# Gate and up of the feed-forwards: the high weight times both activation parts in one 512-column product, the halves added by VectorE

## The chip, the cores and the metric

The kernel runs on one core of a Trainium2 chip. The metric is device time in microseconds of that core, from one launch; the median of three runs is given. A profile is one execution recorded by the hardware profiler.

## The reference, cut to what matters

The reference is a chain of two small networks on 256 tokens of width 1024. The first is two layers of attention and Fourier mixing with modulated norms, for 256 latent and (in layer 0) 256 context tokens; the second is two layers of a recurrent mixer between two feed-forwards. What the change touches is the feed-forward, which all of them share:

```python
FFN_HIDDEN = 2816
def swiglu(h, w_gate, w_up, w_down):
    return (jax.nn.silu(h @ w_gate) * (h @ w_up)) @ w_down
```

It is computed seven times with 256 tokens each: layer 0 of the first network for the latent tokens (call 0) and the context tokens (call 1), layer 1 (call 2), and two in each layer of the second network (calls 3 to 6).

## The kernel before, in words

Activations lie with the feature on the partition: `x`, `h_hi` and so on are 128 partitions x 8 blocks (`KD`, index k) x 256 tokens (`T`). A feed-forward call runs over 22 tiles f (`FT`) of 128 hidden features. For each tile, `gate_up(f)` (L2019) makes two products of 128 hidden features by 256 tokens, gate (part 0) and up (part 1), each summed over the 8 blocks k; `down(f)` (L2035) multiplies the tile's result by 128 rows of the down weight and adds to all 8 output blocks, which stay in PSUM banks 0 to 3 for the whole call.

**Two parts for precision.** TensorE multiplies in the reduced type fp32r. To keep precision, every weight and every activation is split into a high part (rounded to fp32r) and a low part (the rest, in fp32r too), and a product is three: high by high, high weight by low activation, low weight by high activation. That is `split_product` (L2002), with one 256-column product in each of its lines L2005, L2006 and L2007:

```python
nc.tensor.matmul(out, hi, to_hi, start=start, stop=False, skip_group_check=True)
nc.tensor.matmul(out, hi, to_lo, start=False, stop=False, skip_group_check=True)
return nc.tensor.matmul(out, lo, to_hi, start=False, stop=stop, skip_group_check=True)
```

So `gate_up` is 8 x 2 x 3 = 48 products of 256 columns and `down` 8 x 3 = 24. Each comes with a load of its own weight block of 128 x 128 (PEld in the profile). Gate and up of a tile lie in the two halves of one PSUM bank, 4 + f % 2.

**The engines.** SyncE loads the weights in the order of use: `ring_a` holds two chunks of 1 MB (gate and up of one tile), `ring_d` two of 0.5 MB (`load_a` and `load_d`, L493 and L498); a slot is loaded again when `a_used` or `d_used` says that the chunk before last has been split. ScalarE rounds the high parts: `round_a` (L661, `w_hi`, two casts at L668) and `round_d` (L670, `d_hi`, L676). VectorE subtracts for the low parts: `rest_a` (L1307, `w_lo`, L1315) and `rest_d` (L1319, `d_lo`, L1322). GpSimd makes the low part of the activations, `rest_h` (L547, `h_lo`, L552), block by block ahead of a call; in `split_here` (L2009) the first tile of a call waits for each block.

**One tile.** When `gate_up(f)` is done (`gu_done`), ScalarE's `tile(f)` (L696) applies Silu to the gate half, from PSUM into `sg` (L700), and then makes the high parts of tile f+2 and of the down weight f+1. VectorE's `tile(f)` (L1346) multiplies `sg` by the up half from PSUM into `hid` (L1349, `hid_mul`), rounds it (L1353), subtracts (L1355, `hid_ready`), and then makes the low parts of the same weights. All engines work in the order of their own programs; semaphores tie them.

**TensorE's order** in a call (L2056 to L2070) is gate_up(0), gate_up(1), down(0), then gate_up(f), down(f-1) for f = 2 to 21, and down(21) last. So between the end of `gate_up(f)` and `down(f)` lie `down(f-1)` and `gate_up(f+1)`, except for the last tile, where only `down(20)` lies between. `gate_up(f)` waits for `a_used` (its weights are split) and for `hid_mul` of tile f-2 (its bank is read).

**Beside.** In calls 0 and 1, the norms of the other token set are done step by step between the first 12 tiles (`BESIDE`, L72), by `beside(f)` on all three engines; they use PSUM banks 6 and 7, as all norms do (`norm_bank`). These tiles are written out; the others are in a loop of two tiles.

Of the kernel before, what the change touches and what calls it, by code (L numbers as in the profile page):

```python
# [22 lines left out]
F32R = mybir.dt.float32r  # L23
ALU = mybir.AluOpType
# [5 lines left out]
T = 256  # L30
KD = D // P
# [142 lines left out]
def program(nc, wa, wd, c1_in, c2_in, vec_in, small_in, four_in, x_in, ctx_in, out):  # L174
    with ExitStack() as ctx:
        def sb(name, *shape, dtype=F32):
            return ctx.enter_context(nc.sbuf_tensor(name, [P, *shape], dtype))
# [25 lines left out]
        h_hi, h_lo = (sb(n, KD, T, dtype=F32R) for n in ("h_hi", "h_lo"))  # L203
# [63 lines left out]
        def const1(name):  # L267
# [58 lines left out]
            sem(n) for n in ("gu_done", "dn_done", "sg_ready", "hid_mul", "hid_rounded", "hid_ready", "ffn_out"))  # L326
        resid = sem("resid")
# [125 lines left out]
        def wait(eng, semaphore, value, i=None, step=2):  # L453

            if i is not None:
                eng.wait_ge(semaphore, i * step + value)
            elif value > 0:
                eng.wait_ge(semaphore, value)

# [138 lines left out]
        def _(act):  # L598
# [91 lines left out]
            def ffn(call, beside=None):  # L690
# [5 lines left out]
                def tile(f, i=None):  # L696
                    t = call * FT + f
                    wait(act, gu_done, t + 1, i)
                    wait(act, hid_mul, t - 1, i)
                    nc.scalar.activation(sg[:, f % 2, :], ps[:, 4 + f % 2, 0:T], ACT.Silu).then_inc(sg_ready, 1)  # L700
                    if f + 2 < FT:
                        round_a(call, f + 2, i)
                    elif call == 0:
                        round_a(1, f + 2 - FT)
                    if f + 1 < FT:
                        round_d(call, f + 1, i)
                    elif call == 0:
                        round_d(1, 0)

                alone = 2 if beside is None else BESIDE  # L710
# [515 lines left out]
        def _(dve):  # L1226
# [113 lines left out]
            def ffn(call, beside=None):  # L1340
# [5 lines left out]
                def tile(f, i=None):  # L1346
                    t = call * FT + f
                    wait(dve, sg_ready, t + 1, i)
                    nc.vector.tensor_tensor(hid[:, f % 2, :], sg[:, f % 2, :], ps[:, 4 + f % 2, T:2 * T], ALU.mult)\  # L1349
                        .then_inc(hid_mul, 1)  # L1350
# [15 lines left out]
                alone = 2 if beside is None else BESIDE  # L1366
# [560 lines left out]
        def _(pe):  # L1927
# [87 lines left out]

            def ffn(call, key, beside=None):
                c0, d0 = chunk0[f"ffn{call}"], call * FT

                def gate_up(f, i=None):  # L2019
                    c, t = c0 + f, d0 + f  # L2020
                    wait(pe, a_used, c + 1, i)
                    if f >= 2 or call:
                        wait(pe, hid_mul, t - 1, i)
# [37 lines left out]
                alone = 2 if beside is None else BESIDE  # L2061
# [666 lines left out]
```

## Time and profile before

| | |
|---|---|
| median of the three runs | 2498.73 us |
| the three runs | 2503.24, 2498.30, 2498.73 us |
| span of the profiled execution | 2501.0 us |
| time of that execution outside the span | not given separately |
| TensorE busy, mean granted clock | 2388.0 us (95%), 0.979 |
| weight loads busy | 2209.4 us (88%) |
| VectorE, ScalarE, GpSimd busy | 1287.4, 1053.8, 318.5 us |
| read from HBM | 389.46 MB |

How to read it: the span goes from the first to the last instruction. PE is TensorE's matmuls, PEld its weight loads, which run beside them; DVE is VectorE, ACT ScalarE, POOL GpSimd. A matmul's recorded duration is from its start until its last result is out, and matmuls are pipelined: the next starts while results of the one before still come. What one costs in a row is the distance between starts. `128*128 128x256` is a weight block of 128 rows by 128 columns and 256 moving columns. The clock is the share of full speed (2.4 GHz) that was granted to TensorE; it has two levels, 1.0 and 0.5. `A <-B 3.9` is idle time before A that B ended.

### The profile page before, as it was taken

The numbers are of one execution on the slowest core, as the hardware profiler recorded it, in microseconds if no ns is written. First come the engines' busy times: TensorE is split into PE (matmuls) and PEld (weight loads), VectorE is DVE, ScalarE is ACT, GpSimd is POOL, SyncE is SP. The second block draws the span as 40 slices with busy tenths as digits, with TensorE's granted clock in tenths as the row PEclk, the third lists the DMA queues.
The fourth block names the chain that finished last, engine by engine and source line by source line (L and its number), as shares of the span: only waits on it lengthen the run. The fifth ranks groups of instructions, "written<-read, shape, count | busy, mean of one in ns | idle before, by whom it ended". The sixth has DMA issues, their size and how long they took to land.

```text
span 2501.0 us, 51373 instructions
## 1 busy us (share of the span) xinstructions
PE 2388.0 (95%) x21244; PEld 2209.4 (88%) x21244; DVE 1287.4 (51%) x2054; ACT 1053.8 (42%) x1666; POOL 318.5 (13%) x263
## 2 busy tenths in 40 slices
PE   7989999999998799999999999999999999999998
PEld 3756899999975699989998889999999988989998
DVE  1053365565425255465557755555555558555554
ACT  3154444444335343343346434433433355435333
POOL 0000000000000000010014426200100125336000
PEclk9999999999999899999999999999999999999999
DMA  6255454445426355355433213645444232125542
GB/s 264 72 203 219 180 195 177 182 171 177 149 85 236 135 203 186 140 181 185 175 109 125 89 70 119 223 177 179 170 180 176 104 133 101 69 86 182 197 176 101
DMA packets 65512, 392.51 MB, mean 157 GB/s; under 512 B 7264, under 2 KB 7392, under 8 KB 28000
## 3 DMA queue, kind: packets, MB, share of 16 engines
q1 hardware_dynamic: 64224, 383.81, 42.1%
q10 hardware_dynamic: 864, 5.16, 0.5%
q8 instruction: 105, 1.72, 0.3%
q0 software_dynamic: 288, 1.57, 0.2%
q14 instruction: 31, 0.25, 0.0%
HBM read 389.46 MB, written 1.05 MB: 156 GB/s over the span
## 4 chain that ended last, share of the span: by engine, by line
PE 83%; DVE 4%; POOL 4%; issue 4%; ACT 3%; DMA 2%; POOLq 0%; SPq 0%; DVEq 0%; ACTq 0%
PE ps L2005 21%; PE ps L2006 21%; PE ps L2007 21%; PE ps L2091 5%; POOL t_lo L574 3%; PE ps L2106 2%; PE ps L2405 2%; PE ps L2546 1%; POOL h_lo L552 1%; PE ps L1975 1%; DMA ring_a<-in_wa 1%; PE ps L1952 1%; PE ps L2121 1%; DVE work L1395 1%; DMA work<-in_wa 1%
## 5 line engine op out<-in xcount | busy, mean ns | idle before, releaser
L2005 PE MATMUL ps<-h_hi,w_hi 128*128 128x256 f32 x2464 | 701.9, 285 | 7.1 <-DVE mod L1243 2.9
L2006 PE MATMUL ps<-h_lo,w_hi 128*128 128x256 f32 x2464 | 698.7, 284 | 0.0
L2007 PE MATMUL ps<-h_hi,w_lo 128*128 128x256 f32 x2464 | 698.6, 284 | 0.0
L2005 PEld LDWEIGHTS ps<-h_hi,w_hi 128*128 128x128 f32 x2464 | 474.3, 193 | 11.6 <-issue 4.6
L2006 PEld LDWEIGHTS ps<-h_lo,w_hi 128*128 128x128 f32 x2464 | 474.4, 193 | 0.1
L2007 PEld LDWEIGHTS ps<-h_hi,w_lo 128*128 128x128 f32 x2464 | 474.4, 193 | 0.0
L1315 DVE TENSOR_TENSOR w_lo<-ring_a,w_hi 128x1024 fp32r<-128x1024 f32 x308 | 366.4, 1231 | 25.3 <-ACT w_hi L668 25.2
L2005 PE MATMUL ps<-hid_hi,d_hi 128*128 128x256 f32 x1232 | 348.7, 283 | 0.0
L2006 PE MATMUL ps<-hid_lo,d_hi 128*128 128x256 f32 x1232 | 348.7, 283 | 0.0
L2007 PE MATMUL ps<-hid_hi,d_lo 128*128 128x256 f32 x1232 | 348.6, 283 | 0.0
L1349 DVE TENSOR_TENSOR hid<-sg,ps 128x256 f32<-128x256 f32 x154 | 64.9, 421 | 546.9 <-ACT sg L700 546.9
L700 ACT ACTIVATE sg<-ps 128x256 f32<-128x256 f32 x154 | 59.1, 384 | 674.4 <-PE ps L2007 674.4
L668 ACT CAST w_hi<-ring_a 128x1024 fp32r<-128x1024 f32 x308 | 306.0, 1044 | 11.8 <-DMA ring_a<-in_wa 11.8
L2005 PE MATMUL ps<-h_hi,t_hi 128*128 128x256 f32 x880 | 261.3, 297 | 17.9 <-POOL t_lo L574 10.7
L2006 PE MATMUL ps<-h_lo,t_hi 128*128 128x256 f32 x880 | 253.5, 288 | 0.0
L2007 PE MATMUL ps<-h_hi,t_lo 128*128 128x256 f32 x880 | 253.1, 288 | 0.0
L552 POOL TENSOR_TENSOR h_lo<-nsq,h_hi 128x256 fp32r<-128x256 f32 x72 | 60.7, 865 | 1446.8 <-ACT h_hi L687 853.8
L2005 PEld LDWEIGHTS ps<-hid_hi,d_hi 128*128 128x128 f32 x1232 | 236.5, 192 | 0.0
L2006 PEld LDWEIGHTS ps<-hid_lo,d_hi 128*128 128x128 f32 x1232 | 236.5, 192 | 0.0
L2007 PEld LDWEIGHTS ps<-hid_hi,d_lo 128*128 128x128 f32 x1232 | 236.5, 192 | 0.0
L574 POOL TENSOR_TENSOR t_lo<-ring_a,t_hi 128x512 fp32r<-128x512 f32 x120 | 172.6, 1462 | 314.7 <-ACT t_hi L997 314.7
L676 ACT CAST d_hi<-ring_d 128x1024 fp32r<-128x1024 f32 x154 | 161.6, 1050 | 98.4 <-PE ps L2007 98.4
(308 smaller groups left out, 3477.6 us busy)
## 6 DMA issues: line engine op xcount, KB each, us to landing
ring_a<-in_wa SPq DMA_DIRECT2D x282, 1024.0 KB, 4.8
ring_d<-in_wd SPq DMA_DIRECT2D x154, 512.0 KB, 5.3
work<-in_wa SPq DMA_DIRECT2D x6, 1024.0 KB, 22.1
work<-in_small POOLq DMA_DIRECT2D x2, 768.0 KB, 5.5
c<-in_c ACTq DMA_DIRECT2D x1, 1175.0 KB, 10.7
work<-in_c ACTq DMA_DIRECT2D x1, 1088.0 KB, 4.9
x<-in_x ACTq DMA_DIRECT2D x1, 1024.0 KB, 15.1
work<-in_ctx ACTq DMA_DIRECT2D x1, 1024.0 KB, 19.6
```

Of the source, the lines that this page charges most:

```text
L552: nc.gpsimd.tensor_tensor(h_lo[:, k, :], nsq[:, k, :], h_hi[:, k, :].bitcast(F32), ALU.subtract)\
L574: nc.gpsimd.tensor_tensor(t_lo[:, t % 2, k], ring_a[:, c % 2, t % 2, k], t_hi[:, t % 2, k].bitcast(F32), ALU.subtract).then_inc(done, 1)
L668: nc.scalar.copy(w_hi[:, f % 2, part], ring_a[:, c % 2, part]).then_inc(hi_a, 1)
L676: nc.scalar.copy(d_hi[:, f % 2], ring_d[:, d % 2]).then_inc(hi_d, 1)
L700: nc.scalar.activation(sg[:, f % 2, :], ps[:, 4 + f % 2, 0:T], ACT.Silu).then_inc(sg_ready, 1)
L1315: ins = nc.vector.tensor_tensor(w_lo[:, f % 2, part], ring_a[:, c % 2, part], w_hi[:, f % 2, part].bitcast(F32), ALU.subtract)
L1349: nc.vector.tensor_tensor(hid[:, f % 2, :], sg[:, f % 2, :], ps[:, 4 + f % 2, T:2 * T], ALU.mult)\
L2005: nc.tensor.matmul(out, hi, to_hi, start=start, stop=False, skip_group_check=True)
L2006: nc.tensor.matmul(out, hi, to_lo, start=False, stop=False, skip_group_check=True)
L2007: return nc.tensor.matmul(out, lo, to_hi, start=False, stop=stop, skip_group_check=True)
L2091: mm = nc.tensor.matmul(ps[:, 4 + p % 2, 0:cols.stop - cols.start], ring_a[:, slot, i % 2, k, :], h[:, k, cols], start=(k == 0), stop=(k = ...
L2106: mm = nc.tensor.matmul(ps[:, 4 + p % 2, b * P:(b + 1) * P], h[:, k, b * P:(b + 1) * P], ring_a[:, slot, i % 2, k, :], start=(k == 0), sto ...
```

## The change

High and low part of the activations come to lie side by side for each k (`h_parts`, 8 x 2 x 256), so that one product of the high weight with both is 512 columns wide and fills a whole PSUM bank: the first half holds high by high, the second half high weight by low activation. The product of the low weight by the high activation (256 columns) is added onto the second half. Gate and up of a tile now need a bank each: banks 4 and 5 for even tiles, 6 and 7 for odd ones. VectorE adds the two halves, with one `reduce_sum` over pairs that lie 256 elements apart for gate (into `sg`) and one for up (into `hid`); ScalarE applies Silu to `sg` in place, and VectorE multiplies in SBUF. `down` is not changed. Since banks 6 and 7 serve the norms beside calls 0 and 1, the first 12 tiles of these two calls keep the form of before; two more of their tiles are written out ahead of the loop. `wide_from[call]` is the first wide tile, 12 for calls 0 and 1 and 0 for the others.

```diff
--- before.py
+++ after.py
@@ -200,7 +200,8 @@
         vfirst = sb("vfirst", QT, T)
 
 
-        h_hi, h_lo = (sb(n, KD, T, dtype=F32R) for n in ("h_hi", "h_lo"))
+        h_parts = sb("h_parts", KD, 2, T, dtype=F32R)
+        h_hi, h_lo = h_parts[:, :, 0, :], h_parts[:, :, 1, :]
         t_hi, t_lo = (sb(n, 2, KD, P, dtype=F32R) for n in ("t_hi", "t_lo"))
         with nc.sbuf_tensor("work", [P, WORK], F32) as work:
             pass
@@ -324,6 +325,7 @@
         dn_bank, h2_lat = sem("dn_bank"), sem("h2_lat")
         gu_done, dn_done, sg_ready, hid_mul, hid_rounded, hid_ready, ffn_out = (
             sem(n) for n in ("gu_done", "dn_done", "sg_ready", "hid_mul", "hid_rounded", "hid_ready", "ffn_out"))
+        gate_summed, up_summed = sem("gate_summed"), sem("up_summed")
         resid = sem("resid")
         rope_rot, rope_sin, rope_cos, rope_out = (sem(n) for n in ("rope_rot", "rope_sin", "rope_cos", "rope_out"))
         fo_dft, fo_fu, fo_ch, fo_fm, fo_w, fo_out = (
@@ -456,6 +458,15 @@
                 eng.wait_ge(semaphore, i * step + value)
             elif value > 0:
                 eng.wait_ge(semaphore, value)
+
+        def both_parts(bank):
+            return ps[:, bank, :].rearrange("p (a t) -> p t a", t=T)
+
+        wide_from = [BESIDE if call < 2 else 0 for call in range(len(ffns))]
+        wide0 = [sum(FT - w for w in wide_from[:call]) for call in range(len(ffns))]
+
+        def gate_up_bank(f):
+            return 4 + 2 * (f % 2)
 
         def norm_bank(key):
             return 6 + n_id[key] % 2
@@ -695,9 +706,13 @@
 
                 def tile(f, i=None):
                     t = call * FT + f
-                    wait(act, gu_done, t + 1, i)
-                    wait(act, hid_mul, t - 1, i)
-                    nc.scalar.activation(sg[:, f % 2, :], ps[:, 4 + f % 2, 0:T], ACT.Silu).then_inc(sg_ready, 1)
+                    if f >= wide_from[call]:
+                        wait(act, gate_summed, wide0[call] + f - wide_from[call] + 1, i)
+                        nc.scalar.activation(sg[:, f % 2, :], sg[:, f % 2, :], ACT.Silu).then_inc(sg_ready, 1)
+                    else:
+                        wait(act, gu_done, t + 1, i)
+                        wait(act, hid_mul, t - 1, i)
+                        nc.scalar.activation(sg[:, f % 2, :], ps[:, 4 + f % 2, 0:T], ACT.Silu).then_inc(sg_ready, 1)
                     if f + 2 < FT:
                         round_a(call, f + 2, i)
                     elif call == 0:
@@ -707,7 +722,7 @@
                     elif call == 0:
                         round_d(1, 0)
 
-                alone = 2 if beside is None else BESIDE
+                alone = 2 if beside is None else BESIDE + 2
                 for f in range(alone):
                     tile(f)
                     if beside is not None:
@@ -1345,9 +1360,19 @@
 
                 def tile(f, i=None):
                     t = call * FT + f
-                    wait(dve, sg_ready, t + 1, i)
-                    nc.vector.tensor_tensor(hid[:, f % 2, :], sg[:, f % 2, :], ps[:, 4 + f % 2, T:2 * T], ALU.mult)\
-                        .then_inc(hid_mul, 1)
+                    if f >= wide_from[call]:
+                        s, bank = wide0[call] + f - wide_from[call], gate_up_bank(f)
+                        wait(dve, gu_done, t + 1, i)
+                        nc.vector.reduce_sum(sg[:, f % 2, :], both_parts(bank), AX_X).then_inc(gate_summed, 1)
+                        nc.vector.reduce_sum(hid[:, f % 2, :], both_parts(bank + 1), AX_X).then_inc(up_summed, 1)
+                        wait(dve, up_summed, s + 1, i)
+                        wait(dve, sg_ready, t + 1, i)
+                        nc.vector.tensor_tensor(hid[:, f % 2, :], sg[:, f % 2, :], hid[:, f % 2, :], ALU.mult)\
+                            .then_inc(hid_mul, 1)
+                    else:
+                        wait(dve, sg_ready, t + 1, i)
+                        nc.vector.tensor_tensor(hid[:, f % 2, :], sg[:, f % 2, :], ps[:, 4 + f % 2, T:2 * T], ALU.mult)\
+                            .then_inc(hid_mul, 1)
                     wait(dve, hid_mul, t + 1, i)
                     wait(dve, dn_done, t - 1, i)
                     nc.vector.tensor_copy(hid_hi[:, f % 2, :], hid[:, f % 2, :]).then_inc(hid_rounded, 1)
@@ -1363,7 +1388,7 @@
                     elif call == 0:
                         rest_d(1, 0)
 
-                alone = 2 if beside is None else BESIDE
+                alone = 2 if beside is None else BESIDE + 2
                 for f in range(alone):
                     tile(f)
                     if beside is not None:
@@ -2013,12 +2038,35 @@
                 else:
                     pe.wait_ge(norm_out, n_id[key] + 1)
 
+            def wide_gate_up(key, f):
+
+                for k in range(KD):
+                    if f == 0:
+                        split_here(key, k)
+                    for part in range(2):
+                        out = ps[:, gate_up_bank(f) + part, :].rearrange("p (a t) -> p a t", t=T)
+                        nc.tensor.matmul(out, w_hi[:, f % 2, part, k, :], h_parts[:, k], start=(k == 0), stop=False,
+                                         skip_group_check=True)
+                        mm = nc.tensor.matmul(out[:, 1, :], w_lo[:, f % 2, part, k, :], h_hi[:, k, :], start=False,
+                                              stop=(k == KD - 1), skip_group_check=True)
+                return mm
+
             def ffn(call, key, beside=None):
                 c0, d0 = chunk0[f"ffn{call}"], call * FT
 
                 def gate_up(f, i=None):
                     c, t = c0 + f, d0 + f
                     wait(pe, a_used, c + 1, i)
+                    if f >= wide_from[call]:
+                        s = wide0[call] + f - wide_from[call]
+                        if f < 2:
+                            wait(pe, hid_mul, t - 1)
+                        elif f == wide_from[call]:
+                            wait(pe, hid_mul, t)
+                        else:
+                            wait(pe, up_summed, s if f == wide_from[call] + 1 else s - 1, i)
+                        wide_gate_up(key, f).then_inc(gu_done, 1)
+                        return
                     if f >= 2 or call:
                         wait(pe, hid_mul, t - 1, i)
                     for k in range(KD):
@@ -2058,7 +2106,7 @@
                 if call == 1:
                     pe.wait_ge(ffn_out, 1)
                 down(0)
-                alone = 2 if beside is None else BESIDE
+                alone = 2 if beside is None else BESIDE + 2
                 for f in range(2, alone):
                     gate_up(f)
                     down(f - 1)
```

## Rows read from the trace of the kernel before

**Rows 1.** The page: busy time, and the chain that ended last, by line.
```profile
PE 2388.0 (95%) x21244; PEld 2209.4 (88%) x21244; DVE 1287.4 (51%) x2054; ACT 1053.8 (42%) x1666; POOL 318.5 (13%) x263
...
PE 83%; DVE 4%; POOL 4%; issue 4%; ACT 3%; DMA 2%; POOLq 0%; SPq 0%; DVEq 0%; ACTq 0%
PE ps L2005 21%; PE ps L2006 21%; PE ps L2007 21%; PE ps L2091 5%; POOL t_lo L574 3%; PE ps L2106 2%; PE ps L2405 2%; PE ps L2546 1%; POOL h_lo L552 1%; PE ps L1975 1%; DMA ring_a<-in_wa 1%; PE ps L1952 1%; PE ps L2121 1%; DVE work L1395 1%; DMA work<-in_wa 1%
```

**Rows 2.** Windows: stretch, its length, busy us (instructions) by engine, clock, DMA share, GB/s.
```profile
900.00:1000.00 100.00, 100.00 (x836) 100.00 (x835) 53.56 (x69) 37.68 (x46) 0.00 (x0) 1.00 0.49 178
```

**Rows 3.** Timeline of TensorE: start us, duration us, engine, line, operation.
```profile
1203.21 0.28 PE L2006 MATMUL ps<-h_lo,w_hi 128*128 128x256 f32 x1
1203.33 0.28 PE L2007 MATMUL ps<-h_hi,w_lo 128*128 128x256 f32 x1
```

**Rows 4.** The page's groups: the first of the three products of gate and up.
```profile
L2005 PE MATMUL ps<-h_hi,w_hi 128*128 128x256 f32 x2464 | 701.9, 285 | 7.1 <-DVE mod L1243 2.9
```

**Rows 5.** Timeline of the weight loads around one-column products.
```profile
341.92 0.53 PEld L1984 LDWEIGHTS ps<-c,nrt 128*128 128x128 f32 x4
342.37 0.19 PEld L2005 LDWEIGHTS ps<-h_hi,w_hi 128*128 128x128 f32 x1
342.48 0.19 PEld L2006 LDWEIGHTS ps<-h_lo,w_hi 128*128 128x128 f32 x1
```

**Rows 6.** Timeline of TensorE: fp32 products in a row (merged), and one product's own time.
```profile
48.83 3.60 PE L2091 MATMUL ps<-work,ring_a 128*128 128x512 f32 x8
...
109.82 7.42 PE L2106 MATMUL ps<-ring_a,work 128*128 128x128 f32 x65
```

**Rows 7.** Timeline and window of a call's start at the low clock.
```profile
867.17 0.41 PE L2006 MATMUL ps<-h_lo,w_hi 128*128 128x256 f32 x1
867.39 0.41 PE L2007 MATMUL ps<-h_hi,w_lo 128*128 128x256 f32 x1
...
862.00:876.00 14.00, 9.71 (x63) 9.21 (x63) 7.18 (x14) 12.86 (x22) 5.87 (x8) 0.74 0.10 28
```

**Rows 8.** Timeline of TensorE where the next product has another shape in the array.
```profile
1269.57 0.28 PE L2007 MATMUL ps<-hid_hi,d_lo 128*128 128x256 f32 x1
1269.78 0.42 PE L1975 MATMUL ps<-nsq,c 128*32 128x256 f32 x4
...
1334.20 0.38 PE L2346 MATMUL ps<-work 128*128 128x256 f32 x1
1334.51 0.48 PE L2347 MATMUL ps<-work 32*128 32x256 f32 x1
```

**Rows 9.** Timeline of TensorE, first tiles of calls 5 and 2, with idle time.
```profile
1788.44 0.39 PE L2005 MATMUL ps<-h_hi,w_hi 128*128 128x256 f32 x1 [0.18 <-POOL h_lo L552]
...
874.55 0.39 PE L2005 MATMUL ps<-h_hi,w_hi 128*128 128x256 f32 x1 [1.39 <-DVE w_lo L1315]
```

**Rows 10.** Timeline of VectorE over one tile, with the idle time before it.
```profile
1204.14 0.42 DVE L1349 TENSOR_TENSOR hid<-sg,ps 128x256 f32<-128x256 f32 x1 [3.89 <-ACT sg L700]
...
1205.36 2.35 DVE L1315 TENSOR_TENSOR w_lo<-ring_a,w_hi 128x1024 fp32r<-128x1024 f32 x2
1207.63 1.22 DVE L1322 TENSOR_TENSOR d_lo<-ring_d,d_hi 128x1024 fp32r<-128x1024 f32 x1
```

**Rows 11.** Groups of VectorE's reductions, by shape: busy us, mean ns of one.
```profile
L1395 DVE TENSOR_REDUCE work<-ps 128x1 f32<-128x512 f32 x32 | 22.1, 691 | 1.1
...
L1395 DVE TENSOR_REDUCE work<-ps 128x1 f32<-128x256 f32 x16 | 6.7, 418 | 15.8 <-PE ps L2147 15.8
...
L1812 DVE TENSOR_REDUCE work<-ps 128x4 f32<-128x256 f32 x8 | 3.4, 420 | 5.9 <-PE ps L2546 5.9
```

**Rows 12.** Timelines of ScalarE, VectorE and TensorE around the last tile of the last call.
```profile
2485.65 0.38 ACT L700 ACTIVATE sg<-ps 128x256 f32<-128x256 f32 x1 [4.66 <-PE ps L2007]
...
2486.86 0.42 DVE L1355 TENSOR_TENSOR hid_lo<-hid,hid_hi 128x256 fp32r<-128x256 f32 x1
...
2488.33 0.28 PE L2005 MATMUL ps<-hid_hi,d_hi 128*128 128x256 f32 x1
```


## The prediction

> **What bounds the kernel now.** I read the page's busy shares and the chain that ended last first. TensorE is busy 2388.0 of 2501.0 us and holds 83% of the chain, and the three products of `split_product` hold 21% each [rows 1]. So time comes off only where TensorE's own products get shorter, or where it starts to wait. Then a steady stretch inside one feed-forward (FFN) call: in 100 us TensorE is busy 100.00 us with 836 products, VectorE 53.56, ScalarE 37.68, at granted clock 1.00, and the DMA engines work 0.49 of the time [rows 2]. That is 100/836 = 119.6 ns per product, and the timeline shows starts exactly 0.12 us apart [rows 3]. A tile of an FFN call is 48 products of `gate_up` and 24 of `down`: 72 x 0.12 = 8.64 us. The change touches `gate_up`; 2464 of each of its three products were recorded, 7 x 22 x 16 [rows 4].
>
> So everything hangs on one question: what are the 120 ns made of? 256 columns at 2.4 GHz are 106.7 ns, so 13.3 ns are something else.
>
> - *A weight load alone.* Where the products have one column, weight loads follow each other at (0.53 - 0.19) / 3 = 0.113 us, and the first load of `w_hi` behind them needs 0.11 us until the next [rows 5]. A load is thus shorter than 120 ns; it does not explain them alone.
> - *Plain fp32 products.* They take two cycles per column: 512 columns (3.60 - 0.59) / 7 = 0.430 us, 128 columns (7.42 - 0.27) / 64 = 0.1117 us (the last one's own duration goes off: 0.38 at 256 columns [rows 8], 0.21 more and 0.11 less at twice and half the columns) [rows 6]. From 128 to 512 columns that is 0.83 ns per column, just 2 / 2.4, and beyond the columns 3 to 5 ns. So with these the columns are pure clock cycles and what comes on top is a constant.
> - *At the low clock* the fp32r products stand 0.21 us apart in a stretch whose mean granted clock is 0.74, where the clock sits at its 1.2 GHz level: 256 / 1.2 = 213 ns and nothing on top [rows 7]. The extra 13 ns don't scale with the clock and hide behind slower columns.
> - *Without a load beside it.* Where the next product has another shape in the array, its start comes 0.21 us after an fp32r product of 256 columns, and 0.31 us after an fp32 one [rows 8]. The fp32 one streams 213 ns, so 0.097 us is the changeover, and the fp32r one streamed about 0.113 us. So an fp32r product has 6.6 ns on top by itself and another 6.7 with a weight load beside it.
>
> Not shown by any row: whether those 13.3 ns come once per product or grow with its columns. No fp32r product of 512 columns is in the trace.
>
> **The change, part by part.**
>
> *Products.* Per k and part, three loads and three products (360 ns) become two: one of 512 columns, one of 256. Wide tiles: 7 calls x 22 = 154, less the first 12 of calls 0 and 1, so 130; each has 8 x 2 = 16 such triples, 2080 in all. The narrow product stays at 120 ns (it has the same columns and a load beside it). The wide one, bounded from both sides:
>  - lowest, the columns and the 3 ns of an fp32 product, 213 + 3 = 216: saves 24 ns;
>  - once per product, 213.3 + 13.3 = 226.7: saves 13.3 ns;
>  - the first 256 columns beside a load, the rest without, 120 + 113.3 = 233: saves 6.7 ns;
>  - twice the present one, 240: saves nothing.
>
> I take 226.7, because the fp32 rows show pure columns and a constant; a mechanism that charges per column would be a new kind. 2080 x 13.3 ns = **27.7 us**.
>
> Here a rule speaks for more: the Trainium skill (TensorE: Matmul & The Clock Gate, Back-to-back issue gap) gives the gap as columns / 2.4 plus 2.5 ns, 216 ns at 512 columns. By it the saving would be 2080 x 24 = 50 us. By the same rule 256 columns would take 109 ns, where the trace has 120; the measurement decides, and the rule is left as a rival.
>
> *Where the saving is lost.* The first tile of a call waits for the activation parts. In call 5 TensorE stood idle 0.18 us for the last `h_lo`, and in call 2 the second tile waited 1.39 us for `w_lo` [rows 9]; call 6 looks like call 5. There a faster first tile only waits longer: 3 x 16 x 13.3 ns = 0.6 us lost.
>
> *VectorE.* Now per tile from the multiply at 1204.14 to the end of `d_lo` at 1208.85, without a pause: 4.71 us [rows 10]. The change adds two reductions of 512 elements from PSUM. The nearest row is the maximum over 512, 0.691 us; with 4 results instead of 1 it costs 2 ns more at 256 elements, under 1 ns per result, so 256 results may add up to 0.17 us [rows 11]. A reduction steps 256 elements between the two it adds, which no row shows; if each element took double the 1.07 ns of the two sizes of that row, it would be 1.24 us. Below 0.69 nothing speaks for it. I take 0.69, range to 1.24. The tile then is 4.71 + 1.38 = 6.1 us of the new 8.64 - 16 x 0.0133 = 8.43: covered by TensorE, cost nothing. The cover ends at a reduction of 1.86 us. Queued behind the new wait for `gu_done` on VectorE are `w_lo` of tile f+2 and `d_lo` of f+1, wanted by TensorE one to two tiles later; they end some 1.4 us later, against a pause of 3.9 us that VectorE now has before each multiply [rows 10].
>
> *ScalarE.* Silu waits for `gate_summed`, 0.7 us later than now, reads SBUF, and costs the same 0.38 us [rows 12]. Behind it wait the casts of `w_hi` and `d_hi`, then the loads of both rings, that much later; ScalarE is busy 38% of the stretch and the DMA engines half of it [rows 2]: nothing.
>
> *The chain of a tile, where it is bare.* Inside a call TensorE has a whole `gate_up` between asking for tile f's product and needing it. At the end it has only `down(20)`. Now: Silu starts at 2485.65, `hid_lo` ends at 2487.28 and `down(21)` starts at 2488.33: 1.05 us of slack [rows 12]. New: two reductions one after the other, Silu hidden beside the second, so 0.69 + 0.69 - 0.38 + some 0.1 for waits = 1.1 longer. Late by 0.1 us at most, 7 times: 0.7 us. With a reduction of 1.24 it would be 1.2 us, 8 in all. `gate_up` waits for `up_summed` of f-2, done a tile earlier; at tile 13 of calls 0 and 1 it waits for tile 12's, with `down(11)`'s 2.88 us to cover 1.4 us. No stall. The `beside` calls for tiles 12 and 13, new in the unrolled part, do nothing: their last step is at 11.
>
> *At the low clock* a triple takes 427 + 213 = 640 ns, as now. With some five triples at the start of each of five calls so (an estimate from [rows 7]), 25 x 13.3 ns = 0.3 us of the saving goes.
>
> Sum: -27.7 + 0.6 + 0.7 + 0.3 = **-26 us**. The profiled execution's span is 2501.0 us; the runs shown are 2503.24, 2498.30 and 2498.73, median 2498.73. The span is longer than two of them, so the profiled execution is a slightly slow one; a saving in products is the same in each. Predicted: 2498.7 - 26 = **2472 us**.
>
> **The rivals.**
>
> *A: only the columns count.* The wide product takes 216 ns, since 13 ns now come from a load and a product of equal length, and the wide one outlasts its load. For: the fp32 product with a load beside it has only 3 ns on top. Against: 6.6 ns on top without any load [rows 8]. 2080 x 24.4 = 50.8, less 2: 2450 us. 20%.
>
> *C: part per column.* 233 ns, 2080 x 6.7 = 13.9 less 1: 2486 us. For: the two halves of [rows 8] fit it as well. 15%.
>
> *D: all per column.* 240 ns, the change takes away instructions but no time, and the call ends add 1: 2499 us. For: 120 / 256 and 240 / 512 are as simple a reading; against: the 6.6 ns that vanish without a load. 11%. This is also the case in which the change doesn't shorten TensorE's work at all.
>
> *E: VectorE becomes the bound, slower.* Place: the two reductions in each of 130 tiles. Each adds pairs that lie 1 KB apart in PSUM and writes 256 results. Price: VectorE needs 4.71 + 2r; from r = 1.96 us it is over today's 8.64. At 4 ns per element (r = 0.14 + 512 x 0.004 = 2.19) it is 9.1, 130 x 0.45 = 59 us more: 2558 us. Against: 1.07 ns per element in sequence, and under 1 ns per result [rows 11]; it takes almost four times that. A slow reduction also decides if D holds: at 1.24 us the call ends alone give 8 us, 2507. Together 9%.
> Where the skill bears on E: the Trainium skill (SBUF — State Buffer, Door 1: The DMA port swizzle) says that PSUM has 8-byte lines and that steps beyond them slow matmuls down significantly; of VectorE's reads it says nothing, and no row here shows one.
>
> **How the numbers follow.** My forecast (about 227 ns) has 45%, A 20, C 15, D 11, E 9. The range reaches from A with its last 3 us (2447) to short of D: 2492 takes in C with longer reductions. Left out are D and E, 2 in 10. A measurement of this kernel can tell about 0.2%, 5 us, from no change. Faster by more: forecast, A, C: 0.80. Within: D with a short reduction, 0.11. Slower: 0.09.
>
> **What the profile after would show.** 512-column fp32r products whose successors start 0.227 us later (0.216: A; 0.233: C; 0.240: D), the 256-column ones 0.12; a tile period of 8.43 us; two reductions of 0.69 us per tile; VectorE's pause before a tile still over 1 us; `down(21)` of each call idle for 0.1 us or less, released by `hid_lo`. Wrong if the narrow product no longer takes 120 ns, if the reduction is over 1.24 us, or if TensorE waits inside a call.

## The result, and the profile after

The changed kernel takes 2487.07 us (median of 4, 2482.17 to 2488.66), the one before 2498.57 us (median of 4 by then): ratio 0.9947, 95% interval 0.9931 to 0.9962. The medians differ by 11.5 us, the ratio over all runs makes it 13 us, 0.5%. Measured again later beside other kernels, the ratio was 0.9949 (0.9931 to 0.9966). The forecast was 26 us, to 2472; the range (2447 to 2492) holds the result.

The page, busy times and the chain that ended last, answering to [rows 1]:

```profile
PE 2369.6 (95%) x19164; PEld 2095.1 (84%) x19164; DVE 1449.3 (58%) x2314; ACT 1047.2 (42%) x1666; POOL 319.3 (13%) x263
...
PE ps L2048 19%; PE ps L2030 11%; PE ps L2031 11%; PE ps L2032 11%; PE ps L2050 10%; PE ps L2139 6%; POOL t_lo L585 3%; PE ps L2154 2%; PE ps L2453 2%; DMA ring_a<-in_wa 2%; PE ps L2594 1%; POOL h_parts L563 1%; PE ps L2000 1%; PE ps L1977 1%; PE ps L2169 1%
```

2080 products fewer (21244 to 19164), as counted. A steady stretch, the columns as in [rows 2]:

```profile
1100.00:1200.00 100.00, 100.00 (x661) 91.36 (x660) 68.77 (x95) 39.05 (x48) 0.00 (x0) 1.00 0.51 187
```

TensorE is still busy all of the time and VectorE now 69 of 100 us. So the bound has not moved; the products are where to look. The timeline of TensorE at the end of a `gate_up`, against [rows 3] (L2048 is the wide product, L2050 the narrow one):

```profile
1199.73 0.40 PE L2048 MATMUL ps<-h_parts,w_hi 128*128 128x512 f32 x1
1199.97 0.28 PE L2050 MATMUL ps<-h_parts,w_lo 128*128 128x256 f32 x1
1200.08 0.40 PE L2048 MATMUL ps<-h_parts,w_hi 128*128 128x512 f32 x1
...
1203.26 0.40 PE L2048 MATMUL ps<-h_parts,w_hi 128*128 128x512 f32 x1
1203.50 0.28 PE L2050 MATMUL ps<-h_parts,w_lo 128*128 128x256 f32 x1
1203.62 0.28 PE L2030 MATMUL ps<-hid_hi,d_hi 128*128 128x256 f32 x1
```

From 1199.73 to 1203.26 are ten pairs: 353 ns each. Three separate products took 360; the forecast was 346.7. In nanoseconds the starts go 241, 120, 236, 113, 233, 117 and round again: 1060 for three pairs. `gate_up` takes 5.65 us instead of 5.76, `down` 2.88 as before, and the tile 8.527 us instead of 8.640 (between starts of `gate_up`, in the steady part of a call). That is 0.113 us x 130 = 14.7 us. The two profiled spans differ by 15.2 us.

VectorE over one tile, against [rows 10], and its groups of additions:

```profile
1203.83 0.69 DVE L1366 TENSOR_REDUCE sg<-ps 128x256 f32<-128x512 f32 x1 [2.50 <-PE ps L2050]
1204.43 0.68 DVE L1367 TENSOR_REDUCE hid<-ps 128x256 f32<-128x512 f32 x1
1205.15 0.42 DVE L1370 TENSOR_TENSOR hid<-sg,hid 128x256 f32<-128x256 f32 x1
```

```profile
L1366 DVE TENSOR_REDUCE sg<-ps 128x256 f32<-128x512 f32 x130 | 89.9, 692 | 302.4 <-PE ps L2050 302.4
L1367 DVE TENSOR_REDUCE hid<-ps 128x256 f32<-128x512 f32 x130 | 88.5, 681 | 0.0
```

0.69 and 0.68 us: 256 results and steps of 1 KB in PSUM cost nothing over a maximum of 512 elements [rows 11]. In a row they start 0.60 us apart (1203.83 to 1204.43): the second begins before the last results of the first are out. The pause before the tile is 2.5 us instead of 3.9. And the last tile of the last call, against [rows 12]:

```profile
2470.37 0.69 DVE L1366 TENSOR_REDUCE sg<-ps 128x256 f32<-128x512 f32 x1 [3.29 <-PE ps L2050]
2472.48 0.42 DVE L1380 TENSOR_TENSOR hid_lo<-hid,hid_hi 128x256 fp32r<-128x256 f32 x1
```

```profile
2472.92 0.28 PE L2032 MATMUL ps<-hid_hi,d_lo 128*128 128x256 f32 x1
2473.05 0.36 PE L2030 MATMUL ps<-hid_hi,d_hi 128*128 128x256 f32 x1
2473.24 0.28 PE L2031 MATMUL ps<-hid_lo,d_hi 128*128 128x256 f32 x1
```

`hid_lo` ends at 2472.90 and `down(21)` starts at 2473.05, 0.13 us after the product before it and followed after 0.19: it is met just in time and loses less than 0.1 us.

### The profile page after: what moved, and what is told of

The parts are those of the page before. It is cut to its first block, busy times and chain, and to the rows that moved or that the text cites. A ratio compares the mean times of both kernels' runs of the same rounds, so it can differ in the third digit from the quotient of the medians.

```text
span 2485.8 us, 47529 instructions
## 1 busy us (share of the span) xinstructions
PE 2369.6 (95%) x19164; PEld 2095.1 (84%) x19164; DVE 1449.3 (58%) x2314; ACT 1047.2 (42%) x1666; POOL 319.3 (13%) x263
## 3 DMA queue, kind: packets, MB, share of 16 engines
HBM read 389.46 MB, written 1.05 MB: 157 GB/s over the span
## 4 chain that ended last, share of the span: by engine, by line
PE 82%; DVE 4%; POOL 4%; issue 4%; ACT 3%; DMA 2%; POOLq 0%; SPq 0%; DVEq 0%; ACTq 0%
PE ps L2048 19%; PE ps L2030 11%; PE ps L2031 11%; PE ps L2032 11%; PE ps L2050 10%; PE ps L2139 6%; POOL t_lo L585 3%; PE ps L2154 2%; PE ps L2453 2%; DMA ring_a<-in_wa 2%; PE ps L2594 1%; POOL h_parts L563 1%; PE ps L2000 1%; PE ps L1977 1%; PE ps L2169 1%
## 5 line engine op out<-in xcount | busy, mean ns | idle before, releaser
L2048 PE MATMUL ps<-h_parts,w_hi 128*128 128x512 f32 x2080 | 742.1, 399 | 4.8 <-DVE mod L1258 2.9
L2050 PE MATMUL ps<-h_parts,w_lo 128*128 128x256 f32 x2080 | 584.9, 281 | 0.0
L2048 PEld LDWEIGHTS ps<-h_parts,w_hi 128*128 128x128 f32 x2080 | 391.9, 188 | 96.7 <-DVE mod L1258 3.2
L2050 PEld LDWEIGHTS ps<-h_parts,w_lo 128*128 128x128 f32 x2080 | 394.1, 189 | 0.1
L2030 PE MATMUL ps<-h_parts,t_hi 128*128 128x256 f32 x880 | 260.8, 296 | 17.4 <-POOL t_lo L585 10.6
L1366 DVE TENSOR_REDUCE sg<-ps 128x256 f32<-128x512 f32 x130 | 89.9, 692 | 302.4 <-PE ps L2050 302.4
L2031 PE MATMUL ps<-h_parts,t_hi 128*128 128x256 f32 x880 | 252.8, 287 | 0.0
L2032 PE MATMUL ps<-h_parts,t_lo 128*128 128x256 f32 x880 | 252.5, 287 | 0.0
L563 POOL TENSOR_TENSOR h_parts<-nsq,h_parts 128x256 fp32r<-128x256 f32 x72 | 61.4, 876 | 1435.1 <-ACT h_parts L698 849.3
L1337 DVE TENSOR_TENSOR d_lo<-ring_d,d_hi 128x1024 fp32r<-128x1024 f32 x154 | 190.1, 1235 | 11.5 <-ACT d_hi L687 8.9
L2030 PEld LDWEIGHTS ps<-h_parts,t_hi 128*128 128x128 f32 x880 | 172.2, 196 | 25.9 <-issue 13.6
L2031 PEld LDWEIGHTS ps<-h_parts,t_hi 128*128 128x128 f32 x880 | 173.0, 197 | 0.1
## 6 DMA issues: line engine op xcount, KB each, us to landing
x<-in_x ACTq DMA_DIRECT2D x1, 1024.0 KB, 15.2
```

Source lines behind the costliest of these rows:

```text
L563: nc.gpsimd.tensor_tensor(h_lo[:, k, :], nsq[:, k, :], h_hi[:, k, :].bitcast(F32), ALU.subtract)\
L1337: nc.vector.tensor_tensor(d_lo[:, f % 2], ring_d[:, d % 2], d_hi[:, f % 2].bitcast(F32), ALU.subtract)\
L1366: nc.vector.reduce_sum(sg[:, f % 2, :], both_parts(bank), AX_X).then_inc(gate_summed, 1)
L2048: nc.tensor.matmul(out, w_hi[:, f % 2, part, k, :], h_parts[:, k], start=(k == 0), stop=False, skip_group_check=True)
L2050: mm = nc.tensor.matmul(out[:, 1, :], w_lo[:, f % 2, part, k, :], h_hi[:, k, :], start=False, stop=(k == KD - 1), skip_group_check=True)
```

## The experiments

Two theories stood at the start. C, the prediction's rival: every fp32r column costs 0.4427 ns and every load 6.7 ns more, since 233.3 + 120 is just the 353.3 seen. F, the forecast: 13.3 ns once per product, and something else adds 6.6. All times are beside runs of the kernel before on the same chip.

**1. The wide product split again.**

```diff
-                        nc.tensor.matmul(out, w_hi[:, f % 2, part, k, :], h_parts[:, k], start=(k == 0), stop=False,
+                        nc.tensor.matmul(out[:, 0, :], w_hi[:, f % 2, part, k, :], h_hi[:, k, :], start=(k == 0), stop=False,
+                                         skip_group_check=True)
+                        nc.tensor.matmul(out[:, 1, :], w_hi[:, f % 2, part, k, :], h_lo[:, k, :], start=False, stop=False,
```

> The wide product as two of 256 columns with the same weight (48 products per tile again), everything else as in the changed kernel: own banks, two additions, Silu in place. Theory C (each fp32r column costs 0.4427 ns, each weight load beside a product 6.7 ns more) and theory F (13.3 ns once per product, and something about the two halves of the wide product costs 6.6 more) both expect starts 120 ns apart, a tile of 8.63 us, and the time of the kernel before within 4 us: then the additions cost nothing and the whole gain is the removed load. If the new banks or VectorE's additions cost anything on the path, it is over 2503.

2501.48 us where before was 2502.39; ratio 0.9989 (0.9975 to 1.0003). Starts 120 ns apart, `gate_up` 5.76 us, tile 8.640. The two additions are in it (0.69 and 0.68 us) and cost nothing that can be measured; the banks neither. The whole gain is in the products.

**2. 384 columns.**

```diff
-                        nc.tensor.matmul(out, w_hi[:, f % 2, part, k, :], h_parts[:, k], start=(k == 0), stop=False,
-                                         skip_group_check=True)
+                        cols = h_parts[:, k].rearrange("p a t -> p (a t)")[:, 0:384]
+                        nc.tensor.matmul(ps[:, gate_up_bank(f) + part, 0:384], w_hi[:, f % 2, part, k, :], cols,
+                                         start=(k == 0), stop=False, skip_group_check=True)
```

> The wide product cut to 384 columns (the low activation part counts for the first 128 tokens only; the rest of that term is left out). Mean distance of a pair (wide and narrow start to the next wide start): theory C 384 x 0.4427 + 6.7 + 120 = 296.7 ns. Theory F with 6.6 ns for every further 256 columns begun: 160 + 13.3 + 6.6 + 120 = 300 ns. Theory F without that (constant 13.3, forecast): 293.3 ns.

2367.99 us (one run). The timeline:

```profile
1119.96 0.34 PE L2049 MATMUL ps<-h_parts,w_hi 128*128 128x384 f32 x1
...
1121.42 0.34 PE L2049 MATMUL ps<-h_parts,w_hi 128*128 128x384 f32 x1
```

Five pairs in 1.46 us; over a whole `gate_up` 4.696 us / 16 = 293.5 ns. That is the forecast's 293.3, and C's 296.7 is out: from 256 to 384 columns each column costs a clock cycle and nothing else.

**3. All products with 512 columns.**

```diff
-                        mm = nc.tensor.matmul(out[:, 1, :], w_lo[:, f % 2, part, k, :], h_hi[:, k, :], start=False,
+                        mm = nc.tensor.matmul(out, w_lo[:, f % 2, part, k, :], h_parts[:, k], start=False,
```

> The low weight multiplies both activation parts too (adds the low by low term), so all products of gate and up have 512 columns. Theory C: 2 x (226.6 + 6.7) = 466.7 ns per pair, a tile of 16 x 466.7 + 24 x 120 = 10.35 us. Theory F with 6.6 per further 256 columns: the same. Forecast's size (226.7 each): 453.3 ns. If the narrow product behind a wide one was what cost 6.7 ns more: 2 x 226.7 or less.

2697.1 us (one run). The timeline:

```profile
1100.04 0.39 PE L2048 MATMUL ps<-h_parts,w_hi 128*128 128x512 f32 x1
1100.27 0.39 PE L2050 MATMUL ps<-h_parts,w_lo 128*128 128x512 f32 x1
1100.50 0.39 PE L2048 MATMUL ps<-h_parts,w_hi 128*128 128x512 f32 x1
1100.72 0.39 PE L2050 MATMUL ps<-h_parts,w_lo 128*128 128x512 f32 x1
1100.95 0.39 PE L2048 MATMUL ps<-h_parts,w_hi 128*128 128x512 f32 x1
```

0.91 us for four, in nanoseconds 227, 227, 226: exactly the 226.7 that I had taken for the wide product. So the price was right for wide products in a row and, in the stretch shown, wrong for wide and narrow ones in turn. The first few wide products after the 256-column ones of `down` take longer (234, 236, 228, 232, 231) until the row settles. That made a new theory, S: the extra belongs to the change from one length to the other.

**4. The additions twice.**

```diff
+                        wait(dve, spared, 2 * s, i, 4)
+                        nc.vector.reduce_sum(spare[:, 0, :], both_parts(bank), AX_X).then_inc(spared, 1)
                         nc.vector.reduce_sum(sg[:, f % 2, :], both_parts(bank), AX_X).then_inc(gate_summed, 1)
+                        nc.vector.reduce_sum(spare[:, 1, :], both_parts(bank + 1), AX_X).then_inc(spared, 1)
                         nc.vector.reduce_sum(hid[:, f % 2, :], both_parts(bank + 1), AX_X).then_inc(up_summed, 1)
```

> Each of VectorE's two additions is done twice (the extra results go nowhere), 1.4 us more VectorE work per wide tile. If the additions are covered by TensorE inside a call: tile unchanged at 8.53 us, VectorE busy about 84 of 100 us, and only the last tile of each call is late: the chain is 1.4 us longer with about 0 of slack, so up to 7 x 1.4 = 10 us over the changed kernel's 2487. If they were not covered: 130 x 1.4 = 180 us more.

2493.45 us where before was 2502.39; ratio 0.9963 (0.9947 to 0.9978). In its steady stretch VectorE is busy 83 of 100 us and the tile is no longer than 8.527 us (8.526). Of TensorE's idle time, by what ended it:

```profile
  DVE hid_lo L1385: 7.3, 7
```

Seven waits for `hid_lo`, 7.3 us: the call ends, 1.0 us of idle time each, and nothing inside the calls. Counted between starts, `down(21)` comes 1.32 us after the product before it (1263.30 to 1264.62), where the changed kernel has 0.13:

```profile
1263.30 0.28 PE L2037 MATMUL ps<-hid_hi,d_lo 128*128 128x256 f32 x1
1264.62 0.36 PE L2035 MATMUL ps<-hid_hi,d_hi 128*128 128x256 f32 x1 [1.04 <-DVE hid_lo L1385]
```

It is 1.2 us later, and 1.2 us is what two more additions take at 0.60 us from start to start, not the 1.4 of the expectation. So at the call's end the chain of a tile had no slack left, and inside the calls a doubling is still covered. Of the ratio's difference to 0.9947 (0.0016, 4 us) the intervals leave anything from nothing to 10 us.

**5 and 6. The same products, grouped.** With `high(k, part)` the wide product and `low(k, part)` the narrow one, as before:

```diff
                 for k in range(KD):
                     if f == 0:
                         split_here(key, k)
                     for part in range(2):
+                        high(k, part)
+                for k in range(KD):
+                    for part in range(2):
+                        mm = low(k, part)
```

> The same products in another order: in each tile first all 16 wide ones, then all 16 narrow ones. Found so far: 120 ns each for 256 columns in a row, 226.7 each for 512 in a row (13.3 once per product, as forecast), but 353.2 for a pair of 512 and 256 in turn, 6.6 more than the sum. Theory S (the 6.6 ns belong to the alternation, once per pair): a tile's gate and up take 16 x 226.7 + 16 x 120 = 5.55 us instead of 5.65, and the kernel 2080 x 6.6 = 13.7 us less than the changed one: some 2474 where before is 2500. Theory C (per column, 233.3 + 120): no change, 2487.

2481.66 us where before was 2502.03; ratio 0.9916 (0.9895 to 0.9936). A tile's 32 products, merged by the timeline into two rows:

```profile
1125.82 3.82 PE L2047 MATMUL ps<-h_parts,w_hi 128*128 128x512 f32 x16
1129.48 2.08 PE L2051 MATMUL ps<-h_parts,w_lo 128*128 128x256 f32 x16
```

The wide ones take 3.66 us (16 x 226.7 would be 3.63; the rest is the settling), the narrow ones (2.08 - 0.28) / 15 = 0.120 us. `gate_up` is 5.567 us and the tile 8.447, 0.08 less than in the changed kernel, 10.4 us over 130 tiles; S wanted 13.7. The whole time is 7.7 us over S's 2474. Part of that lies at the start of calls 4 to 6. With all wide products first, TensorE asks for the last block of the activations much sooner and stands idle for it, here in call 5:

```profile
1772.76 0.73 PE L2047 MATMUL ps<-h_parts,w_hi 128*128 128x512 f32 x2 [0.74 <-POOL h_parts L563]
1774.42 0.73 PE L2047 MATMUL ps<-h_parts,w_hi 128*128 128x512 f32 x2 [0.93 <-POOL h_parts L563]
```

Such waits of gate and up add to 6.5 us in this trace, 1.5 us in the changed kernel's and 1.5 us in that of the next order. The other kernel groups within a block k (wide gate, wide up, narrow gate, narrow up):

> For each block k wide gate, wide up, narrow gate, narrow up: half as many alternations. Theory S: 350 ns per pair, a tile's gate and up 5.60 us, 7 us less than the changed kernel. Theory C: no change.

2479.37 us; ratio 0.9906 (0.9882 to 0.9931). Its timeline:

```profile
1124.33 0.62 PE L2047 MATMUL ps<-h_parts,w_hi 128*128 128x512 f32 x2
1124.79 0.40 PE L2051 MATMUL ps<-h_parts,w_lo 128*128 128x256 f32 x2
1125.03 0.63 PE L2047 MATMUL ps<-h_parts,w_hi 128*128 128x512 f32 x2
...
1125.72 0.63 PE L2047 MATMUL ps<-h_parts,w_hi 128*128 128x512 f32 x2
```

Two blocks, four pairs, in 1.39 us: 348 ns per pair; `gate_up` 5.573 us, 6 ns longer than fully grouped, where S wanted 5.60. Over the plain sum of 5.547 us a tile's gate and up take 0.10 us with 16 alternations (the changed kernel), 0.026 with 8 and 0.020 with one. So S's fixed 6.6 ns per alternation is out, though the order does matter. The two orders can't be told apart by their times. Both lie below the changed kernel's 0.9947 and 0.9949 by the medians, but the latter was taken on another chip and the 95% intervals meet (0.9931 to 0.9962 against 0.9895 to 0.9936 and 0.9882 to 0.9931). The tile shows the gain plainly: 8.527, 8.447 and 8.453 us.

**7. 448 columns.**

```diff
-                        nc.tensor.matmul(out, w_hi[:, f % 2, part, k, :], h_parts[:, k], start=(k == 0), stop=False,
-                                         skip_group_check=True)
+                        cols = h_parts[:, k].rearrange("p a t -> p (a t)")[:, 0:448]
+                        nc.tensor.matmul(ps[:, gate_up_bank(f) + part, 0:448], w_hi[:, f % 2, part, k, :], cols,
+                                         start=(k == 0), stop=False, skip_group_check=True)
```

> The wide product cut to 448 columns (low activation part for 192 tokens only). With 384 columns the pair was 293.5 ns, the forecast's 160 + 13.3 + 120. Theory S as it stands doesn't say why 384 is free of the extra: if it belongs to 512 alone (a whole bank), the pair is 186.7 + 13.3 + 120 = 320 ns; if it grows between 384 and 512, 323; if any alternation above some width has it whole, 326.7.

2416.16 us (one run):

```profile
1119.89 0.36 PE L2049 MATMUL ps<-h_parts,w_hi 128*128 128x448 f32 x1
...
1121.17 0.36 PE L2049 MATMUL ps<-h_parts,w_hi 128*128 128x448 f32 x1
```

Four pairs in 1.28 us, 320 ns: no extra at all, though wide and narrow alternate. Of the widths tried (256, 384, 448, 512) only 512 in turn with 256 has it.

**8. The narrow product onto the other half.** `out[:, 1, :]` becomes `out[:, 0, :]` in the narrow product.

> The narrow product is added onto the first half of the bank instead of the second (the sum of the halves is the same). If the extra 6.6 ns come from adding onto columns that the wide product wrote last, it goes: 346.7 ns per pair, tile 8.43 us. Otherwise the pair stays at 353.

2494.57 us (one run); `gate_up` 5.65 us, starts 241, 120, 236, 113 as in the changed kernel. Which columns are added onto plays no part.

**9. Other operands.** The grouped order with

```diff
-                    nc.tensor.matmul(out_of(part), w_hi[:, f % 2, part, k, :], h_parts[:, k], start=(k == 0), stop=False,
+                    nc.tensor.matmul(ps[:, gate_up_bank(f) + part, :], bf_w[:, :], bf_h[:, :], start=(k == 0), stop=False,
```

and the same two bf16 tiles in the narrow product.

> The grouped order (16 wide, 16 narrow per tile) with bf16 operands of a constant in place of weights and activations in gate and up, so their values are left out; loads and columns as many as before. If the 13.3 ns over the columns belong to fp32r (4 bytes per element): starts 216 ns apart at 512 columns and about 109 at 256, gate and up of a tile 5.20 us, kernel about 2481 - 130 x 0.36 = 2434. If they come with any product and its load: 226.7 and 120, 5.57 us, 2481.

2433.61 us (one run), the 2434 of the first case:

```profile
1123.83 3.40 PE L2052 MATMUL ps<-bf_h,bf_w 128*128 128x512 bf16 x15
1127.07 1.91 PE L2056 MATMUL ps<-bf_h,bf_w 128*128 128x256 bf16 x16
```

15 starts in 3.24 us are 216 ns (one of the 16 records is missing in the trace), and the narrow ones are 109 ns apart. Only some 2.5 ns stand over the columns, so the 13.3 don't come with just any product and its load. The run changed the type and, with it, let all products read the same two constant tiles. That the type makes the difference is the likely reading, but the two weren't separated. Nor was the moving operand from the weight with its load.

**10. 128 columns.** In the grouped order the narrow product becomes `out_of(part)[:, 1, 0:P]` from `h_hi[:, k, 0:P]`.

> Grouped order, the narrow products with 128 columns instead of 256 (the low weight's term is left out for the second 128 tokens). The forecast's rule alone: 53.3 + 13.3 = 66.7 ns apart. If a weight load sets a floor: 111 to 113 ns as between one-column products, or 120 if the load itself is what takes 120 beside an fp32r product. Rival A of the prediction (the 120 ns come from loads) wants 120; the forecast wants the floor of 111 to 113.

2472.93 us (one run):

```profile
1121.26 3.85 PE L2047 MATMUL ps<-h_parts,w_hi 128*128 128x512 f32 x16
1124.95 1.90 PE L2051 MATMUL ps<-h_parts,w_lo 128*128 128x128 f32 x16
```

In nanoseconds the narrow starts are 109 to 115 apart after the first, 112 in the mean: the loads' own pace, as between one-column products [rows 5]. A load of fp32r weights doesn't take 120 ns, so the 120 of the kernel before was not the load's pace; halving the columns gives only 8 ns where 53 were taken off.

**11. The same form in the mixer.** Grouped order in the feed-forwards, and in the mixer's projection tiles

```diff
-                        mm = split_product(ps[:, bank + t % 2, 0:T],
-                                           (t_hi[:, t % 2, k, :], t_lo[:, t % 2, k, :], h_hi[:, k, :], h_lo[:, k, :]),
-                                           start=(k == 0), stop=(k == KD - 1))
+                        nc.tensor.matmul(ps[:, bank + t % 2, :].rearrange("p (a t) -> p a t", t=T), t_hi[:, t % 2, k, :],
+                                         h_parts[:, k], start=(k == 0), stop=False, skip_group_check=True)
+                    for k in range(KD):
+                        mm = nc.tensor.matmul(ps[:, bank + t % 2, T:2 * T], t_lo[:, t % 2, k, :], h_hi[:, k, :], start=False,
+                                              stop=(k == KD - 1), skip_group_check=True)
```

> Grouped order in the feed-forwards, and the mixer's 110 projection tiles in the same form: 8 wide products, then 8 narrow ones, in a whole bank. Only the first half of the bank is read after, so the two terms with a low part are left out; it measures what the form would be worth there without the additions. If TensorE bounds these tiles: 880 x 13.3 = 11.7 us less than the grouped kernel, some 2469. If GpSimd's splitting of the weights bounds most of them (TensorE idled some 11 us for it before): under half of that.

(The form reached 94 of the 110 tiles.) 2484.59 us; ratio 0.9916 (0.9899 to 0.9934), the grouped kernel's own: nothing gained. The first mixer's stretch, here and then in the grouped kernel:

```profile
1262.00:1566.40 304.40, 287.73 (x3060) 250.72 (x3060) 186.49 (x280) 143.30 (x216) 133.93 (x99) 0.96 0.31 109
```

```profile
1261.10:1563.10 302.00, 286.47 (x3436) 269.08 (x3436) 186.66 (x280) 143.27 (x216) 133.49 (x100) 0.98 0.31 110
```

376 products fewer, and the stretch is 2.4 us longer at a lower granted clock. TensorE's group there waits for the split weights:

```profile
L2377 PE MATMUL ps<-h_parts,t_hi 128*128 128x512 f32 x752 | 210.8, 420 | 18.4 <-POOL t_lo L585 12.9 <-POOL h_parts L563 3.5 <-issue 1.9
```

What TensorE gained it waited for at GpSimd. That this is why nothing came out is read from these rows, not tried.

**12. The changed kernel again.**

> The changed kernel itself once more, beside the others on one chip: 0.9947 of the kernel before as measured first (2489 where before is 2502), against 0.9916 and 0.9906 of the two reordered kernels. If the reordering gained nothing, all three would agree.

2491.03 us where before was 2503.59: ratio 0.9949 (0.9931 to 0.9966), `gate_up` 5.65 us again.

This trace and the first one of the same kernel show one thing more. The first two tiles of call 3 are 32 pairs in turn, with no `down` between. Nine pairs of them, in the first execution and then in this one:

```profile
1073.51 0.40 PE L2048 MATMUL ps<-h_parts,w_hi 128*128 128x512 f32 x1
...
1076.63 0.39 PE L2048 MATMUL ps<-h_parts,w_hi 128*128 128x512 f32 x1
```

```profile
1073.44 0.40 PE L2048 MATMUL ps<-h_parts,w_hi 128*128 128x512 f32 x1
...
1076.62 0.40 PE L2048 MATMUL ps<-h_parts,w_hi 128*128 128x512 f32 x1
```

3.12 us and 3.18 us: 346.7 ns per pair (the starts go 230, 117 all along) and 353.3 (241, 120, 236, 113, 233, 117). It is the same kernel, the same order of products and the full clock in both. So the plain sum can be had with 512 and 256 in turn too, and the extra is a rhythm into which the products fall or don't. Call 5 starts at 346.7 in both traces, the other calls at either or in between. In the wide tiles behind a call's first two, where `gate_up` and `down` take turns, both traces have 353 throughout.

## Why the prediction was right or wrong

**The bound** was right: TensorE is busy all of a steady stretch before and after, and the time came off its products alone (experiment 1).

**The step that failed** is the price of the wide product, "once per product, 213.3 + 13.3 = 226.7: saves 13.3 ns", together with "The narrow product stays at 120 ns". The pair was forecast at 346.7 ns and took 353.0 over a whole `gate_up` (5.648 us / 16). It saved 7.0 ns instead of 13.3, and 2080 of them made 14.6 us instead of 27.7. The term was mis-sized by half, and this is nearly the whole error: with 7.0 ns the sum of the prediction is 14.6 less 1.6, 13.0 us, against 11.5 between the medians and 13 by the ratio.

**The constant behind the price was right all the same.** From 256 to 512 columns 13.3 ns come once per product: 120 ns at 256, 293.5 for the pair at 384, 320 at 448, 226.7 at 512 in a row (experiments 2, 3, 7). What the prediction didn't have is that 512 and 256 in turn mostly cost 6.6 ns more per pair than each in its own row. In some first tiles of a call they don't, and there the pair takes just the 346.7 ns of the forecast (experiment 12). No row of the kernel before could show it, since all its fp32r products were alike; the prediction priced each product alone and then set them in turn.

**Rival C** named the measured time (2486) for a wrong reason. Its 233.3 + 120 fits the pair to 0.3 ns; 384 columns, the wide products in a row and the stretches at 346.7 refuted it (experiments 2, 3, 12). Its hit is luck: a number that fits is no proof. It came from splitting [rows 8] into 6.6 ns alone and 6.7 with a load. That split takes the changeover as equally long for two different following products, which no run tested.

**Rival A** (216 ns) fell with the wide products in a row at 226.7 and with the loads' pace of 112 ns (experiments 3 and 10). By the Trainium skill (TensorE: Matmul & The Clock Gate, Back-to-back issue gap) the gap is columns / 2.4 plus 2.5 ns, which it gives for an isolated product; the bf16 products here agree (216 and 109 ns), though they come in a row, and the fp32r ones take 13.3 instead of 2.5. For a row of loads and products the same section of the Trainium skill gives about 131 ns at 512 columns, and no run here agrees with that (216 and 226.7 ns). The prediction put the first to a row of products and did not mention the second. **Rival D** (nothing gained) and **rival E** (VectorE as the bound) are out: the additions take 0.69 and 0.68 us, and even done twice they stay covered.

**VectorE and ScalarE**: right that all of it is covered inside a call, and the addition was sized right (0.69 forecast, 0.69 and 0.68 measured). At a call's end two terms were off and made up for each other. From the first instruction behind `gate_up` to the end of `hid_lo` it is 2.53 us (2470.37 to 2472.90) instead of 1.63, so 0.9 longer and not 1.1, since the additions start 0.60 us apart. And the slack was 0.9 and not 1.05, since TensorE starts 0.15 us after the end of `hid_lo`. The loss, below 0.1 us per call, came out as forecast. Doubling showed that the slack is used up to the last: 1.2 us later, seven times. Silu took 0.42 us from SBUF, not the 0.38 of PSUM, which cost nothing.

**The first tiles**: two of the three kept their wait. In call 6 TensorE waited 0.17 us for the last `h_lo` before and waits 0.33 us now, and in call 2 the wait for `w_lo` is 1.31 us instead of 1.39 [rows 9]:

```profile
2293.17 0.50 PE L2048 MATMUL ps<-h_parts,w_hi 128*128 128x512 f32 x1 [0.33 <-POOL h_parts L563]
```

```profile
870.77 0.50 PE L2048 MATMUL ps<-h_parts,w_hi 128*128 128x512 f32 x1 [1.31 <-DVE w_lo L1330]
```

Call 5 didn't wait this time and call 4 did, so which call is caught is not fixed. The prediction left out call 1, whose first tile has the old form: it waits 0.89 us for the last low part where it waited 0.27, and 0.88 in experiment 12's trace. Why is open.

**Still open**: why 512 and 256 in turn mostly cost more, what puts them into one rhythm or the other, and why 448 and 256 never do. It isn't the half that is added onto (experiment 8). 512 columns also fill a whole bank, and which of the two matters wasn't separated. An order of three or four of a kind, or 512 in turn with 384, wasn't tried.

## What to carry to other kernels

Price a product by the spacing that a row of equal products shows, and remember that the order can have a price too: here 32 products of two lengths took 5.65 us in turn and 5.57 grouped, and the ratio was 0.9947 in turn, 0.9916 and 0.9906 grouped. Grouping two and two was enough here; with all sixteen wide ones first, TensorE waited for inputs that come block by block. A product merged into its neighbour, with its weight load, was worth at most its constant (13.3 ns of 120), since the loads ran beside the products anyway. And a shorter product pays only where TensorE is what the others wait for; in the mixer, where GpSimd splits the weights, the same form gave nothing.

## What the runs showed of the hardware that was not expected

- fp32r products of 512 and 256 columns in turn: 353.3 ns per pair in most tiles, 346.7 in some, in two executions of one kernel at the same place; in rows of their own 226.7 + 120 = 346.7. 448 and 256 in turn: 320, the plain sum. After 256-column products, about five 512-column ones pass (234, 236, 228, 232, 231 ns) before they settle at 226.7.
- fp32r products of 256 to 512 columns carry 13.3 ns over their columns at the full clock, bf16 ones of one constant tile 2.5.
- An addition of pairs that lie 1 KB apart in PSUM, 256 results from 512 elements, takes 0.69 us, as long as one maximum over 512 elements in sequence; in a row the next starts after 0.60 us.
